# Two transformer blocks on one core: the 32-byte offset of the first projection's activations, and the placement of the tables around them

## The chip, the core and the metric

The kernel runs on one core of a Trainium2 chip. The metric is the device time of one execution in microseconds (us). Before the change it is 1629.65 us, the median of three runs (1628.27 to 1630.36).

The engines are TensorE (PE, with its weight loads shown apart as PEld), VectorE (DVE), ScalarE (ACT), GpSimd (POOL) and SyncE (SP, which here only issues transfers). On-chip memory (SBUF) has 128 partitions; an address below is the byte offset within a partition. A matmul has a stationary operand, which a weight load (LDWEIGHTS) puts into the array, and a moving operand, which streams through it. The profile names a matmul as `ps<-moving,stationary`.

## The reference

One sequence of 256 tokens with 2048 channels goes through two blocks, in float32. Cut to the products that carry the time:

```
h    = rms(x) * (1 + scale) + shift          # scale, shift, gate = silu(c) @ w_ada + b_ada
proj = h @ w_in                              # 2048 x 8192: q, k, v, z of attention; q, f, i, z of the recurrence
x    = x + gate * (concat(attention, recurrence) @ w_out)
z    = rms(x) @ w_in_2                       # second block; also rms(mem) @ w_mem_kv_2
x    = x + concat(pool, mla, cross) @ w_o_2
x    = x + (silu(conv(rms(x) @ w_gate)) * (rms(x) @ w_up)) @ w_down
```

Every large product is computed from split operands: weights and activations are each cut into a high and a low part of type fp32r, and three products (high·high, high·low, low·high) are added up in PSUM.

## The kernel before, in words

**Weights.** The weights come in pieces of 1 MB (128 partitions x 2048 values, 256 pieces) and the pieces of `w_ada` in the same size (36 through the same ring, 12 through a buffer `side`). SP loads them into a ring `raw` of 4 slots. Each piece is two halves of 1024 columns. For each half ACT writes the high part into `wh` (line 1488) and DVE the low part into `wl` (line 1886); both are rings of 4 halves. PE waits for the low part (semaphore `s_lo`) before it uses a half, ACT waits for PE before it overwrites one, and SP waits for DVE before it refills a slot of `raw`. The 512 halves are used in a fixed order.

**Activations.** A product reads its activations from one of two buffers of 16 tiles x 512 values: 256 high values of a tile, then its 256 low values. Each buffer has two names: `hA` and `hB`, and `hA2` and `hB2`, which are the same bytes begun 32 bytes later. The table `moving` says which name each stage uses. In the order of the program:

- *Memory rows* (stage B, lines 1278 to 1280, 64 matmuls each): the activations in `hB` are stationary, the weights move, 512 columns a matmul.
- *Chunks* (stage A, lines 1185 to 1187, function `chunk`): the first half of `w_in`, columns for v, the recurrence's input, q and k. The activations in `hA2` are stationary, the weights move, 512 columns. 64 halves x 12 matmuls = 768 matmuls.
- *Tiles of w_in* (stage A, lines 1138 to 1140, function `s`): the other half of `w_in`. The weights are stationary, the activations in `hA2` move, 256 columns. 32 tiles x 16 x 3 = 1536 matmuls. Between them stand the small matmuls of attention and recurrence.
- *w_out* (stage C, `hB2`), *w_in_2* (stage 2, `hA2`), latent products and *w_o_2* (stages L and D, `hB2`): the same lines 1138 to 1140, weights stationary. One short product here (lines 1161 to 1163, 8 matmuls each) has the activations stationary, from `hB2`.
- *Gate and up* (stage 3, lines 1142 and 1143): weights stationary, `hA2` moves. The high weights take one matmul of 512 columns (high and low activations at once), the low weights one of 256: 1408 pairs.
- *Down* (stage F, lines 1195 to 1197, 352 each): the activations in `hB` are stationary, the weights move, 512 columns.

**Who fills `hA2` in stage A.** ACT writes the high part (line 1547), DVE the low part (line 1940), tile by tile; PE waits for the low part of a tile the first time it reads it.

**Addresses.** The buffers are laid out one behind another in `program`, by the byte counter `at[0]`, from 16512, which is a multiple of 64. All buffers whose sizes are powers of two stay on multiples of 64; a step of 32 bytes, and the odd size of the table `vs`, shift what follows. The remainders of the start addresses, before and after the change:

| buffer | before, mod 64 / mod 128 | after, mod 64 / mod 128 |
|---|---|---|
| `raw`, `wh`, `wl`, `side`, `hA` | 0 / 0 | 0 / 0 |
| `hA2` | 32 / 32 | 32 / 32 |
| `xs` (rows of x, attention's outputs) | 32 / 32 | 0 / 64 |
| `hB` | 0 / 0 | 0 / 64 |
| `hB2`, `early` | 32 / 32 | 32 / 96 |
| `cs` (constants, with the identity) | 32 / 32 | 0 / 0 |
| `vs` (vectors of gains and biases) | 32 / 32 | 0 / 0 |
| `ones` | 0 / 0 | 32 / 96 |
| `cols`, `work` | 32 / 32 | 32 / 96 |

Slices of `hA`, `hB`, `wh` and `wl` that PE reads begin at multiples of 512 bytes from the buffer's start, so they have its remainders.

Of the kernel before, what the change touches and what calls it, by code (L numbers as in the profile page):

```python
# [7 lines left out]
F32 = mybir.dt.float32  # L8
F32R = mybir.dt.float32r
U8 = mybir.dt.uint8  # L10
ALU = mybir.AluOpType
ACT = mybir.ActivationFunctionType
AX = mybir.AxisListType

P = 128
T = 256
D = 2048
# [32 lines left out]
def _layout(table, sizes):  # L50
    at = 0
    for name, n in sizes:
        table[name] = (at, at + n)
        at += n
    return at
# [4 lines left out]
NVEC = _layout(VEC, [("norm_g", 16), ("b_ada", 48), ("g_mix", 16), ("g_ffn", 16), ("g_mem", 16),  # L60
                     ("conv_w", 132), ("conv_b", 44), ("lb", 16), ("pool_scale", 4), ("g_q_lat", 4),
                     ("g_kv_lat", 2), ("q_norm_g", 1), ("k_norm_g", 1), ("hg_norm_g", 1), ("g_q_x", 1),
                     ("g_k_x", 1), ("gq_nope", 1), ("gq_rope", 1), ("gk_nope", 1), ("gk_rope", 1), ("c", 16)])
# [743 lines left out]
class Counts:  # L807
# [8 lines left out]
    def mark(self, task, eng, step):  # L816
        name = f"{self.chain_of(task)}_{eng}"
        self.now[name] += 1
        self.found[task, eng, step] = self.now[name]
        return self.sems[name]  # L820

    def after(self, task, eng, step):
        name = f"{self.chain_of(task)}_{eng}"
        return self.sems[name], 1 if self.table is None else self.table[task, eng, step]


def program(nc, table, wts, ada, xN, xT, memN, crow, cst, vec, msk, wpool, dt, out):
    o = order()
    with ExitStack() as ctx:
        at = [nc.sbuf_base + (-nc.sbuf_base) % 32]  # L830
        ctx.enter_context(nc.sbuf_tensor("slab", [P, (nc.sbuf_top - at[0]) // 4 - 8], F32))

        def sb(name, shape, dtype=F32, size=4):
            t = nc.alloc_sbuf_tensor_at(name, shape, dtype, offset=at[0])
            at[0] += int(np.prod(shape[1:])) * size
            at[0] += (-at[0]) % 32
            return t
# [4 lines left out]
        side = nc.alloc_sbuf_tensor_at("side", [P, 4, D], F32, offset=at[0])  # L842
        hA_off = at[0]
        hA = sb("hA", [P, KT, 512], F32R)
        at[0] += 32
        xs = sb("xs", [P, KT, T])
        vs = sb("vs", [P, NVEC])
        ones = sb("ones", [P, P])
        at[0] += (hA_off - at[0]) % 2048
        early = nc.alloc_sbuf_tensor_at("early", [P, 4096], F32, offset=at[0] + 32)  # L850
        E1 = nc.alloc_sbuf_tensor_at("E1", [P, 512], F32, offset=at[0] + 32 + 15 * 2048)[:, :]
        hB_off = at[0]
        hB = sb("hB", [P, KT, 512], F32R)
        at[0] += 32
        cs = sb("cs", [P, NCST])
        mk = sb("mk", [P, len(LEVELS), P], U8, 1)
        wp = sb("wp", [P, 4, P])
        cols = sb("cols", [P, 224])
        hA2 = nc.alloc_sbuf_tensor_at("hA2", [P, KT, 512], F32R, offset=hA_off + 32)
        hB2 = nc.alloc_sbuf_tensor_at("hB2", [P, KT, 512], F32R, offset=hB_off + 32)  # L860
# [4 lines left out]
        def carve(at, *shape, of=None):  # L865
            n = int(np.prod(shape))
            assert at + n <= (NW if of is None else 4096), (at, n)
            ap = (work if of is None else of)[:, at:at + n]
            if len(shape) == 2:
                ap = ap.rearrange("p (a b) -> p a b", a=shape[0])  # L870
            if len(shape) == 3:
                ap = ap.rearrange("p (a b c) -> p a b c", a=shape[0], b=shape[1])
            return ap, at + n
# [21 lines left out]
        mark, after = counts.mark, counts.after  # L895
# [5 lines left out]
        def v_(name, i=0):  # L901
            a, _ = VEC[name]
            return vs[:, a + i:a + i + 1]
# [13 lines left out]
        xn, _ = carve(base, KT, T)  # L917
# [7 lines left out]
        hf = [ct[:, i, :] for i in range(4)]  # L925
# [49 lines left out]
        for s in range(2):  # L975
            B = {}
# [22 lines left out]
        for _ in range(2):  # L999
            m, a1 = carve(a1, T)  # L1000
            mq.append(m)
        lset = []
        for s in range(4):
            B = {}
# [16 lines left out]
        evs = [b[1] for b in o.beats if b[0] == "ev" and b[1][0] in ("g", "u")]  # L1021
        ev_no = {t: i for i, t in enumerate(evs)}
        ev_last = {"u": "mul"}
        moving = {"A": hA2, "2": hA2, "3": hA2, "B": hB, "C": hB2, "L": hB2, "D": hB2, "F": hB}
        kv_lat = {**{i: ("lkv", 1) for i in (0, 1)}, **{i: ("lq", 3) for i in (8, 9, 10, 11)}}

        def moving_ready(buf, kt):
            if buf == "A":
                return after(("xt", kt), "dve", "lo")
            if buf == "B":  # L1030
                return after(("open",), "dve", ("mlo", kt))
            if buf == "C":
                return after(("gs", kt), "dve", "lo") if kt < 8 else after(("rt", (kt - 8) // 2), "dve", "lo")
            if buf == "2":
                return after(("wo", kt), "dve", "slo")
            if buf == "L":
                return after(kv_lat[kt], "dve", ("lo", kt % 8))
            if buf == "D":
                if kt < 4:
                    return after(("pf", kt), "dve", "lo")  # L1040
                return after(("mla", kt - 4) if kt < 12 else ("mem", kt - 12), "dve", "lo")
            if buf == "3":
                return after(("o2", kt), "dve", "slo")
            return after(("hs", kt), "dve", "lo")
# [16 lines left out]
        def bank_clear(tile):  # L1061
            if tile[0] == "pf":
                return after(tile, "dve", "scale")
            if tile[0] in ("qm", "km"):
                return set_done(*tile)
            if tile[0] in M_TILES:
                return after(tile, "dve" if tile[0] == "mv" else "act", "c1")
            if tile[0] in ACT_TILES:
                return after(tile, "act", "ev")
            return after(tile, "dve", "rm" if tile[0] in RMS_TILES else "add")  # L1070
# [53 lines left out]
        def _(e):  # L1124
# [41 lines left out]
            def chunk(h, g, kt, pair, fresh):  # L1166
                n, kts = GROUPS[g]
                e.wait_ge(s_lo, h + 1)
                if fresh:
                    e.wait_ge(*moving_ready("A", kt))  # L1170
                for i in (1, 0) if g == 0 and kt == kts[0] and pair == 0 else (0, 1):
                    c = 2 * pair + i
                    w1, w2 = wh[:, h % WS, i * 512:(i + 1) * 512], wl[:, h % WS, i * 512:(i + 1) * 512]
                    if kt == kts[0]:
                        if g == 0 and c in (1, 2):
                            e.wait_ge(*after(("open",), "act", ("xc", 7)))
                        elif g == 0:
                            e.wait_ge(*bank_clear(o.prev[SET_TILES[n][c]]))
                        else:
                            e.wait_ge(*after(("part", g - 1), "act" if g < 3 else "dve", c))  # L1180
                    for t in range(2):
                        hi = hA2[:, kt, t * P:(t + 1) * P]
                        lo = hA2[:, kt, T + t * P:T + (t + 1) * P]
                        po = ps[SET_BANKS[c][t]][:, :]
                        e.matmul(po, hi, w1, start=kt == kts[0], stop=False)  # L1185
                        e.matmul(po, hi, w2, start=False, stop=False)  # L1186
                        m = e.matmul(po, lo, w1, start=False, stop=kt == kts[-1])  # L1187
                m.then_inc(s_half)
# [294 lines left out]
        def _(e):  # L1483
# [52 lines left out]
            def x_value(kt):  # L1536
                t = ("xt", kt)
                m, c = mod[:, 16 + kt:17 + kt], mod[:, kt:kt + 1]
                e.wait_ge(*after(("ada", 0, kt), "dve", "ttr"))
                e.activation(m, m, ACT.Identity, scale=v_("norm_g", kt), bias=gb[:, kt:kt + 1]).then_inc(mark(t, "act", "m"))  # L1540
                e.activation(c, c, ACT.Identity, bias=v_("b_ada", kt)).then_inc(mark(t, "act", "c"))
                e.wait_ge(*after(t, "act", "c"))
                e.wait_ge(*after(("open",), "act", ("xc", 7)))
                if kt >= 4:
                    e.wait_ge(*after(("xt", kt - 4), "dve", "lo"))
                e.activation(hf[kt % 4], xn[:, kt, :], ACT.Identity, scale=m, bias=c).then_inc(mark(t, "act", "h"))
                e.activation(hA2[:, kt, 0:T], xn[:, kt, :], ACT.Identity, scale=m, bias=c).then_inc(mark(t, "act", "hi"))

            def bounds():
                t = ("bounds",)  # L1550
# [331 lines left out]
        def _(e):  # L1882
# [54 lines left out]
            def x_low(kt):  # L1937
                t = ("xt", kt)
                e.wait_ge(*after(t, "act", "hi"))
                e.tensor_tensor(hA2[:, kt, T:2 * T], hf[kt % 4], hA2[:, kt, 0:T].bitcast(F32), ALU.subtract).then_inc(mark(t, "dve", "lo"))  # L1940

            def bounds():
                t = ("bounds",)
# [656 lines left out]
```

## Time and profile before

| | |
|---|---|
| median of three runs | 1629.65 us |
| the profiled execution's own time | 1630.36 us |
| its span in the profile | 1628.3 us, 24289 instructions |
| PE busy | 1583.3 us (97%), 9650 matmuls |
| PEld busy | 1403.4 us (86%) |
| DVE busy | 1151.7 us (71%) |
| ACT busy | 860.7 us (53%) |
| POOL busy | 137.7 us (8%) |
| chain that ended last | PE 83%, DVE 9%, ACT 4%, issue 2%, POOL 2% |
| transfers | 331.02 MB, mean 203 GB/s |
| granted TensorE clock over the span | 0.99 of full speed |

The span is the time from the first to the last instruction of the profiled execution; its own time lies 2.1 us above. Matmuls overlap in the profile: each row's duration runs from its start to the arrival of its last result, while the next has long begun. What a matmul costs in a dense stretch is therefore read from one start to the next, not from its duration.

### The profile page before, as it was taken

To read this page: it belongs to the slowest core of one execution; us is meant where nothing else is said; L and a number is where in the kernel's file an instruction comes from. 1 tells how busy PE (TensorE), PEld (TensorE's weight loads), DVE (VectorE), ACT (ScalarE), POOL (GpSimd) and SP (SyncE) were. 2 spreads that over 40 slices of the span, in tenths; PEclk is the share of its full clock that TensorE was granted. 3 is DMA by queue.
4 is the path that set the end of the run, shared out by engine and by line. 5 is a ranking of instruction groups with operands and counts; after the bars stand their busy time and mean duration, and the time that the engine had idled before them with its cause. 6 is when DMAs were issued, how large, how long until landed. Compare 5 with 4: busy or idle time off the path is not lost.

```text
span 1628.3 us, 24289 instructions
## 1 busy us (share of the span) xinstructions
PE 1583.3 (97%) x9650; PEld 1403.4 (86%) x9650; DVE 1151.7 (71%) x1696; ACT 860.7 (53%) x1321; POOL 137.7 (8%) x164
## 2 busy tenths in 40 slices
PE   8999999988999999898999999999999999999999
PEld 6788889987999999886789888888888888888887
DVE  5888858877778976656677777777777777555544
ACT  6766447677665555454556554544444444444442
POOL 0000000312120320031414000000000000000000
PEclk9999999999999999998999999999999999999999
DMA  9999965513556864432234445555545545555552
GB/s 376 357 360 366 380 248 216 207 65 129 198 189 250 326 219 157 152 130 78 104 130 156 167 173 203 185 184 201 194 176 199 196 175 199 207 183 205 185 202 104
DMA packets 47825, 331.02 MB, mean 203 GB/s; under 512 B 5281, under 2 KB 6689, under 8 KB 8417
## 3 DMA queue, kind: packets, MB, share of 16 engines
q1 hardware_dynamic: 45184, 312.20, 52.5%
q0 software_dynamic: 2240, 17.04, 2.7%
q8 instruction: 76, 1.25, 0.3%
q14 instruction: 35, 0.29, 0.1%
q10 hardware_dynamic: 290, 0.25, 0.1%
HBM read 327.37 MB, written 2.10 MB: 202 GB/s over the span
## 4 chain that ended last, share of the span: by engine, by line
PE 83%; DVE 9%; ACT 4%; issue 2%; POOL 2%; ACTq 0%; DVEq 0%; POOLq 0%
PE ps L1142 19%; PE ps L1143 10%; PE ps L1138 6%; PE ps L1140 6%; PE ps L1139 6%; PE ps L1197 5%; PE ps L1195 5%; PE ps L1196 5%; PE ps L1185 4%; PE ps L1187 4%; PE ps L1186 4%; DVE wl L1886 3%; ACT wh L1488 2%; DVE raw L1932 1%; PE ps L1320 1%
## 5 line engine op out<-in xcount | busy, mean ns | idle before, releaser
L1886 DVE TENSOR_TENSOR wl<-raw,wh 128x1024 fp32r<-128x1024 f32 x512 | 624.0, 1232 | 347.9 <-ACT wh L1488 347.5
L1488 ACT ACTIVATE wh<-raw 128x1024 fp32r<-128x1024 f32 x512 | 531.0, 1054 | 365.0 <-PE ps L1197 130.6
L1142 PE MATMUL ps<-hA,wh 128*128 128x512 f32 x1408 | 490.2, 391 | 0.0
L1143 PE MATMUL ps<-hA,wl 128*128 128x256 f32 x1408 | 397.8, 283 | 0.0
L1142 PEld LDWEIGHTS ps<-hA,wh 128*128 128x128 f32 x1408 | 265.0, 188 | 55.6
L1143 PEld LDWEIGHTS ps<-hA,wl 128*128 128x128 f32 x1408 | 266.8, 190 | 0.0
L1138 PE MATMUL ps<-hA,wh 128*128 128x256 f32 x752 | 218.8, 291 | 0.0
L1140 PE MATMUL ps<-hA,wl 128*128 128x256 f32 x752 | 210.5, 280 | 0.0
L1139 PE MATMUL ps<-hA,wh 128*128 128x256 f32 x752 | 210.3, 280 | 0.0
L1138 PE MATMUL ps<-hB,wh 128*128 128x256 f32 x576 | 166.8, 290 | 5.9 <-issue 2.5
L1139 PE MATMUL ps<-hB,wh 128*128 128x256 f32 x576 | 162.6, 282 | 0.0
L1140 PE MATMUL ps<-hB,wl 128*128 128x256 f32 x576 | 162.5, 282 | 0.0
L1138 PEld LDWEIGHTS ps<-hA,wh 128*128 128x128 f32 x752 | 142.1, 189 | 1.8 <-issue 1.2
L1139 PEld LDWEIGHTS ps<-hA,wh 128*128 128x128 f32 x752 | 142.1, 189 | 0.8 <-issue 0.2
L1140 PEld LDWEIGHTS ps<-hA,wl 128*128 128x128 f32 x752 | 141.8, 189 | 0.0
L1195 PE MATMUL ps<-wh,hB 128*128 128x512 f32 x352 | 137.0, 389 | 0.0
L1196 PE MATMUL ps<-wl,hB 128*128 128x512 f32 x352 | 136.9, 389 | 0.0
L1197 PE MATMUL ps<-wh,hB 128*128 128x512 f32 x352 | 136.9, 389 | 0.0
L1138 PEld LDWEIGHTS ps<-hB,wh 128*128 128x128 f32 x576 | 110.1, 191 | 11.4 <-issue 6.0
L1139 PEld LDWEIGHTS ps<-hB,wh 128*128 128x128 f32 x576 | 110.2, 191 | 0.4 <-issue 0.2
L1140 PEld LDWEIGHTS ps<-hB,wl 128*128 128x128 f32 x576 | 110.1, 191 | 0.0
L1185 PE MATMUL ps<-wh,hA 128*128 128x512 f32 x256 | 101.3, 396 | 1.0 <-DVE wl L1886 1.0
(287 smaller groups left out, 2072.7 us busy)
## 6 DMA issues: line engine op xcount, KB each, us to landing
raw<-in_wts SPq DMA_DIRECT2D x256, 1024.0 KB, 4.8
raw<-in_ada SPq DMA_DIRECT2D x36, 1024.0 KB, 5.4
side<-in_ada POOLq DMA_DIRECT2D x12, 1024.0 KB, 8.8
work<-in_memN SPq DMA_DIRECT2D x2, 1024.0 KB, 8.8
xs<-in_xN POOLq DMA_DIRECT2D x1, 2048.0 KB, 19.2
xs<-in_xT POOLq DMA_DIRECT2D x2, 1024.0 KB, 6.2
out_rows<-xs SPq DMA_DIRECT2D x8, 256.0 KB, 2.5
wp<-in_dt SPq DMA_DIRECT2D x8, 128.0 KB, 2.3
```

The source lines that it names most:

```text
L1138: e.matmul(po, w1, hl[:, 0:T], start=first, stop=False)
L1139: e.matmul(po, w1, hl[:, T:2 * T], start=False, stop=False)
L1140: i = e.matmul(po, w2, hl[:, 0:T], start=False, stop=last)
L1142: e.matmul(ps[bank][:, :], w1, hl, start=first, stop=False)
L1143: i = e.matmul(ps[bank][:, T:2 * T], w2, hl[:, 0:T], start=False, stop=last)
L1185: e.matmul(po, hi, w1, start=kt == kts[0], stop=False)
L1186: e.matmul(po, hi, w2, start=False, stop=False)
L1195: e.matmul(po, hi, w1, start=first, stop=False)
L1196: e.matmul(po, hi, w2, start=False, stop=False)
L1197: return e.matmul(po, lo, w1, start=False, stop=last)
L1488: e.activation(wh[:, h % WS, :], raw[:, n % RAW, part * HALF:(part + 1) * HALF], ACT.Copy).then_inc(s_hi)
L1886: e.tensor_tensor(wl[:, h % WS, :], src, wh[:, h % WS, :].bitcast(F32), ALU.subtract).then_inc(s_lo)
```

## The change

The table `moving` gives stage A the name `hA` in place of `hA2`, and the six other places that write or read the buffer in stage A follow: ACT's high part, DVE's low part, and the stationary operands of `chunk`. Stages 2 and 3 stay on `hA2`, and C, L and D on `hB2`.

The layout changes with it. The gap behind `hA` and the one behind `hB` grow from 32 to 64 bytes. `vs` and `ones` move from behind `xs` to places behind `cs` and `wp`. The line that rounded the start of `hB` so that it stood at the same remainder mod 2048 as `hA` is gone; `hB` now starts 64 bytes past that remainder. The order of instructions on every engine, their shapes and their waits are the same; only addresses differ.

```diff
@@ program @@
         hA_off = at[0]
         hA = sb("hA", [P, KT, 512], F32R)
-        at[0] += 32
+        at[0] += 64
         xs = sb("xs", [P, KT, T])
-        vs = sb("vs", [P, NVEC])
-        ones = sb("ones", [P, P])
-        at[0] += (hA_off - at[0]) % 2048
         early = nc.alloc_sbuf_tensor_at("early", [P, 4096], F32, offset=at[0] + 32)
         E1 = nc.alloc_sbuf_tensor_at("E1", [P, 512], F32, offset=at[0] + 32 + 15 * 2048)[:, :]
         hB_off = at[0]
         hB = sb("hB", [P, KT, 512], F32R)
-        at[0] += 32
+        at[0] += 64
         cs = sb("cs", [P, NCST])
+        vs = sb("vs", [P, NVEC])
         mk = sb("mk", [P, len(LEVELS), P], U8, 1)
         wp = sb("wp", [P, 4, P])
+        ones = sb("ones", [P, P])
         cols = sb("cols", [P, 224])
@@ the table of names @@
-        moving = {"A": hA2, "2": hA2, "3": hA2, "B": hB, "C": hB2, "L": hB2, "D": hB2, "F": hB}
+        moving = {"A": hA, "2": hA2, "3": hA2, "B": hB, "C": hB2, "L": hB2, "D": hB2, "F": hB}
@@ PE, chunk @@
-                        hi = hA2[:, kt, t * P:(t + 1) * P]
-                        lo = hA2[:, kt, T + t * P:T + (t + 1) * P]
+                        hi = hA[:, kt, t * P:(t + 1) * P]
+                        lo = hA[:, kt, T + t * P:T + (t + 1) * P]
@@ ACT @@
-                e.activation(hA2[:, kt, 0:T], xn[:, kt, :], ACT.Identity, scale=m, bias=c).then_inc(mark(t, "act", "hi"))
+                e.activation(hA[:, kt, 0:T], xn[:, kt, :], ACT.Identity, scale=m, bias=c).then_inc(mark(t, "act", "hi"))
@@ DVE @@
-                e.tensor_tensor(hA2[:, kt, T:2 * T], hf[kt % 4], hA2[:, kt, 0:T].bitcast(F32), ALU.subtract).then_inc(mark(t, "dve", "lo"))
+                e.tensor_tensor(hA[:, kt, T:2 * T], hf[kt % 4], hA[:, kt, 0:T].bitcast(F32), ALU.subtract).then_inc(mark(t, "dve", "lo"))
```

## Rows read from the trace of the kernel before

**Rows 1.** The page, chain that ended last, shares of the span by engine.
```profile
PE 83%; DVE 9%; ACT 4%; issue 2%; POOL 2%; ACTq 0%; DVEq 0%; POOLq 0%
```

**Rows 2.** Busy us (and count) of each engine by stage, clock, DMA share, GB/s.
```profile
66.00:110.00 44.00, 42.97 (x186) 34.40 (x185) 41.17 (x43) 30.73 (x51) 1.59 (x3) 1.00 0.90 342
110.00:200.00 90.00, 90.00 (x387) 72.55 (x386) 76.20 (x73) 48.03 (x72) 0.00 (x0) 1.00 0.97 375
200.00:249.00 49.00, 49.00 (x211) 39.48 (x210) 29.33 (x33) 21.39 (x23) 0.00 (x0) 1.00 0.68 246
249.00:540.00 291.00, 276.98 (x2258) 268.84 (x2257) 227.36 (x411) 193.06 (x311) 49.53 (x61) 0.99 0.51 184
1385.00:1628.00 243.00, 239.71 (x1058) 198.03 (x1056) 120.96 (x125) 98.98 (x114) 0.00 (x0) 1.00 0.51 182
```

**Rows 3.** Timeline of PE in the chunks: start us, us, engine, line, operands, shape.
```profile
129.81 0.40 PE L1185 MATMUL ps<-wh,hA 128*128 128x512 f32 x1
...
131.21 0.40 PE L1185 MATMUL ps<-wh,hA 128*128 128x512 f32 x1
```

**Rows 4.** Timeline of PE in the down stage.
```profile
1399.84 0.39 PE L1197 MATMUL ps<-wh,hB 128*128 128x512 f32 x1
...
1401.20 0.39 PE L1197 MATMUL ps<-wh,hB 128*128 128x512 f32 x1
```

**Rows 5.** Four lines of PE: count, duration ns min/median/max, first and last start.
```profile
L1185 PE MATMUL ps<-wh,hA x256: 395/396/469, 70.2 to 248.8; 128*128 128x512 f32 x128
...
L1195 PE MATMUL ps<-wh,hB x352: 389/389/473, 1385.1 to 1623.9; 128*128 128x512 f32 x176
...
L1278 PE MATMUL ps<-wh,hB x64: 389/389/796, 16.5 to 68.4; 128*128 128x512 f32 x64
...
L1161 PE MATMUL ps<-wh,hB x8: 395/440/628, 691.6 to 766.4; 128*128 128x512 f32 x8
```

**Rows 6.** Timeline of PE in gate and up.
```profile
899.72 0.39 PE L1142 MATMUL ps<-hA,wh 128*128 128x512 f32 x1
...
900.76 0.39 PE L1142 MATMUL ps<-hA,wh 128*128 128x512 f32 x1
```

**Rows 7.** Timeline of PE in the tiles of w_in.
```profile
259.78 0.28 PE L1139 MATMUL ps<-hA,wh 128*128 128x256 f32 x1
...
263.28 0.28 PE L1139 MATMUL ps<-hA,wh 128*128 128x256 f32 x1
```

**Rows 8.** Waits from 66 to 249 us: who for whom, us in total, times, longest.
```profile
ACT wh L1488 <- DMA raw<-in_wts: 42.3, 15, 5.3
...
ACT wh L1488 <- PE ps L1187: 31.1, 21, 1.7
...
PE ps L1185 <- DVE wl L1886: 1.0, 1, 1.0
```

**Rows 9.** Busy time by stretch: the opening, for the rate of the transfers.
```profile
16.00:66.00 50.00, 49.17 (x228) 40.49 (x228) 40.16 (x52) 35.43 (x50) 5.46 (x10) 1.00 0.98 392
```

**Rows 10.** DVE's halves, near 203 us: start us, us, line, operands.
```profile
202.12 1.23 DVE L1886 TENSOR_TENSOR wl<-raw,wh 128x1024 fp32r<-128x1024 f32 x1 [1.69 <-ACT wh L1488]
```

**Rows 11.** Timeline of PE at the same moment.
```profile
204.71 0.40 PE L1185 MATMUL ps<-wh,hA 128*128 128x512 f32 x1
```

**Rows 12.** Groups by line and shape on DVE: count, busy us, mean ns, idle before.
```profile
L2341 DVE TENSOR_TENSOR hB<-work,hB 128x256 fp32r<-128x256 f32 x44 | 18.5, 421 | 7.7 <-ACT hB L1852 7.7
...
L1940 DVE TENSOR_TENSOR hA<-work,hA 128x256 fp32r<-128x256 f32 x16 | 6.7, 420 | 0.0
```

**Rows 13.** Transposes of xs, 16 in a row: start us, us from first to last.
```profile
53.49 1.91 PE L1264 MATMUL ps<-cs,xs 128*128 128x128 f32 x16
```

**Rows 14.** Waits of PE from 249 to 540 us, the longest two.
```profile
PE ps L1320 <- DVE work L2038: 2.7, 2, 1.7
PE ps L1320 <- ACT work L1598: 2.6, 1, 2.6
```

## Prediction

> **What bounds the kernel now.** I read the chain that ended last first: 83% of it is PE, 9% DVE, 4% ACT [rows 1]. No instruction, shape or wait is changed, only addresses, so the question is whether an address changes how fast an engine goes, and whether that engine is PE where it changes. The table by stage comes next [rows 2]. In the chunks PE is busy 90.00 of 90 us (110 to 200) and 49.00 of 49 (200 to 249); in the tiles of w_in and what goes with them 276.98 of 291; in the down stage 239.71 of 243. Durations of overlapping matmuls don't tell their cost, so the third view is the timeline, where I take the distance of starts in a dense stretch at a granted clock of 1.00 (2.4 GHz):
>
> - chunks: six steps from 129.81 to 131.21, 1.40 / 6 = 233.3 ns for 512 columns [rows 3]. Stationary operand at remainder 32 (mod 64), moving operand at 0.
> - down stage: six steps from 1399.84 to 1401.20, 1.36 / 6 = 226.7 ns for 512 columns [rows 4]. Stationary 0, moving 0.
> - gate and up: three pairs from 899.72 to 900.76, 1.04 / 3 = 346.7 ns for 768 columns [rows 6]. Stationary 0, moving 32.
> - tiles of w_in: 30 steps from 259.78 to 263.28, 3.50 / 30 = 116.7 ns for 256 columns [rows 7]. Stationary 0, moving 32.
>
> Columns alone at 2.4 GHz would take 213.3, 213.3, 320.0 and 106.7 ns. What lies on top is 20.0, 13.3, 26.7 for a pair (13.3 each) and 10.0 ns.
>
> **The first step: a stationary operand at remainder 32 costs 6.7 ns more a matmul.** Chunks and down stage run the same shape, weights at remainder 0 moving in both. They differ in the stationary buffer's remainder, but also in the load beside them (DMA share 0.97 against 0.51, DVE 76.20 of 90 us against 120.96 of 243 [rows 2]). Two other lines part these. The memory rows at 16 to 68 us read `hB` (remainder 0) with a DMA share of 0.98 [rows 9] and have a median of 389 ns, as the down stage has; the eight products of line 1161 read `hB2` (remainder 32) at 692 to 766 us and have a minimum of 395, as the chunks have, with 395 to 396 [rows 5]. So the 6 to 7 ns follow the address and not the neighbours. In the chunks 768 matmuls move from 32 to 0: 768 x (233.3 - 226.7) = 5.1 us, all on PE, which is full there.
>
> The Trainium skill speaks against this step. "SBUF — State Buffer", section "Who interferes with whom", has PE's two read ports independent and says that PE and ACT never wait on anyone; "TensorE: Matmul & The Clock Gate", section "Back-to-back issue gap", gives a gap that depends on columns alone, 512 / 2.4 + 2.5 = 215.8 ns. By these an address costs nothing and the change gives 0. The rows don't agree: none of the 512-column streams is at 215.8, and two that differ in address are 6.7 apart. That rule is a rival below.
>
> **What eats of the 5.1 us: the supply of weights.** From 66 to 200 us the DMA engines are busy 0.90 to 0.97 of the time [rows 2], and ACT waits 42.3 us for pieces of weights, against 31.1 us for PE to free a half [rows 8]. PE itself waits only 1.0 us there [rows 8]. The closest moment is at 204.71 us, when PE begins a half whose low part was ready at 202.12 + 1.23 = 203.35, 1.4 us ahead [rows 10, 11]. At that point some 50 halves of 12 matmuls have gone by, 50 x 12 x 6.7 ns = 4.0 us. If the arrivals stood still, PE would wait 4.0 - 1.4 = 2.6 us there, and never get it back. They don't stand still: part of the ring's pace is PE's own (those 31.1 us), and 375 GB/s must rise only to 375 x 233.3 / 226.7 = 386, which is below the 392 of the opening [rows 9]. Ends 0 and 2.6; I take 0.5, near the lower, because the rate has been shown.
>
> **The second step: the tiles of w_in.** 1536 matmuls keep their stationary operand at 0, while the moving one goes from 32 to 0. No row of before has 256 moving columns at remainder 0. The nearest rows on the role of the moving operand are gate and up against the down stage: moving at 32 and at 0, both 13.3 ns a matmul on top [rows 4, 6]. I take 0. From above: the 10.0 ns could rise to the 20.0 of the chunks, 1536 x 10.0 = 15.4 us. From below: to nothing on top at all, again 15.4 us, now gained; nearer is the 3.3 ns by which 10.0 and 13.3 differ, 5.1 us either way. PE is busy in 95% of this stretch, with waits for DVE and ACT of at most 2.7 us in total each [rows 2, 14], so nearly all of such a step would reach the end.
>
> **The third step: the rest that moves.** `hB` keeps its remainder mod 64 but goes from 0 to 64 mod 128, `hB2` from 32 to 96. If 64 is what counts, nothing happens; all rows stand at 0 or 32, so they can't tell. I take 0, with 8.3 us as the upper end (next part). `ones`, stationary in 88 small matmuls, goes from 0 to 32, `xs`, stationary in 96 transposes, from 32 to 0. At 6.7 ns each that is 0.6 us lost and 0.6 gained, and the transposes, 16 in 1.91 us or some 109 ns apart [rows 13], may be bound by their weight loads, so that nothing comes back. I take 0, ends -0.6 and +0.6. DVE and ACT write the buffer at 0 instead of 32: DVE's sum of 256 columns takes 421 ns into `hB` at remainder 0 and 420 into `hA2` at 32 [rows 12]. Nothing there. Transfers into `xs`, `cs` and `vs` land at another remainder; no row prices that, and they lie in stretches where the engines of the DMA have the weights to bring as well. 0.
>
> **Sum.** -5.1 + 0.5 + 0 + 0 = -4.6 us. The profiled execution took 1630.36 us, 2.1 above its span of 1628.3; by the sum it becomes 1625.8. The median of the runs is 0.7 lower, 1629.65, and becomes 1625.1. I start between them, from 1629.9, and give 1625.3. A difference below 0.2% (3.3 us) is about what a measurement of this kernel can't tell from no change.
>
> **Rivals.**
>
> *A, the moving operand takes it back.* Everything measured with both operands at 0 has 13.3 ns on top. The 256-column stream at moving 32 has only 10.0. If the 10.0 is a merit of the 32 bytes between the two streams, it becomes 13.3 and the tiles go from 116.7 to 120.0: 1536 x 3.3 = 5.1 us lost, against 5.1 gained. For it: the 3.3 ns want an explanation. Against it: gate and up has the same 32 bytes and no such merit. -5.1 + 0.5 + 5.1 = +0.5: 1630.4.
>
> *B, slower.* The same place, another price: the narrow stream, in which weight load and moving columns are equally long, pays the full 6.7 ns when both begin at the same remainder. 1536 x 6.7 = 10.2 us; -5.1 + 0.5 + 10.2 = +5.6: 1635.5. It decides from 4.6 us / 1536 = 3.0 ns a matmul on, that is, above 119.7 ns the kernel is no longer faster at all. Against it: down stage and memory rows have the same remainders for both streams and are the fast ones.
>
> *C, slower by `hB`.* If what counts is the remainder mod 128, the down stage's 1056 and the memory rows' 192 matmuls pay 6.7 ns: 1248 x 6.7 = 8.3 us; -4.6 + 8.3 = +3.7: 1633.6.
>
> *D, both streams gain.* The narrow stream has its 3.3 ns less with an aligned moving operand: -4.6 - 5.1 = -9.7: 1620.2. For it: the chunks show that an operand pays for starting at 32; against it: gate and up again.
>
> *E, an address costs nothing*, the skill's rule, with the 6.7 ns due to something in the chunks that stays. 0: 1629.9. Against it stand lines 1278 and 1161 [rows 5].
>
> **How the numbers follow.** Forecast 0.42, A 0.26, D 0.09, B 0.12, C 0.08, E 0.03. Of the forecast's 0.42 some 0.06 lose over 1.3 us to the supply and end within 0.2%. Faster by over 0.2%: 0.36 + 0.09 = 0.45. Within: 0.06 + 0.26 + 0.03 = 0.35. Slower: 0.12 + 0.08 = 0.20. The forecast's own range is 1624.5 (nothing lost) to 1628 (2.6 lost and 0.6 of small ones). The range for 8 in 10 takes in A and C and most of D's price, and leaves out B: 1620.5 to 1634.
>
> **What would show it.** In the profile after: the chunks' matmuls at 389 ns and 226.7 apart, and the stage some 5 us shorter; if 395 and 233.3 stay, the first step is wrong. PE's waits for DVE at lines 1185 and following, up to 200 us, give the supply's part: 1.0 us now, up to 3.6. The tiles of w_in at 116.7 apart (forecast), 120.0 (A), over 119.7 (B) or below 114 (D). The down stage at 226.7 (forecast) or 233.3 (C). Gate and up must stay at 346.7 a pair. The forecast is wrong if the tiles' distance moves by more than 1 ns or so, since 1536 of them weigh twice as much as the 768 of the chunks.

## The result, and the profile after

The changed kernel takes 1641.01 us, median of four runs (1639.46 to 1643.21), against 1629.97 in the same sitting. The ratio is 1.0062 (95% interval 1.0044 to 1.0080): 10 to 11 us slower, where 4.6 us faster was forecast, and beyond the range.

The profiled execution has a span of 1637.0 us against 1628.3. That execution itself took 1638.8 us, a little less than the four. Where the 8.7 us came in, from the first matmul of a stage to the first of the next, in us; the two right columns belong to experiments below:

| stage | before | after | stage A alone | layout alone |
|---|---|---|---|---|
| opening, memory rows | 70.2 | 70.0 | 70.1 | 70.3 |
| chunks | 179.3 | 179.2 | 177.8 | 179.8 |
| tiles of w_in | 255.7 | 259.4 | 258.9 | 255.5 |
| w_out to w_o_2 | 383.3 | 384.1 | 383.3 | 384.3 |
| gate and up | 496.6 | 494.1 | 495.0 | 494.2 |
| down | 243.2 | 250.2 | 243.2 | 250.1 |
| span | 1628.3 | 1637.0 | 1628.4 | 1634.2 |

Gate and up have the same addresses in all four and still differ by 2.4 us: so much of one profile is no evidence. (So the 0.8 us of the stages from w_out to w_o_2 are none either.) The tiles (+3.7) and the down stage (+7.0) are above it.

The timeline of PE after the change answers to [rows 3, 4, 7]; the lines of the kernel have numbers lower by one. First the chunks and the down stage:

```profile
129.73 0.39 PE L1186 MATMUL ps<-wh,hA 128*128 128x512 f32 x1
...
131.09 0.39 PE L1186 MATMUL ps<-wh,hA 128*128 128x512 f32 x1
...
1399.69 0.39 PE L1195 MATMUL ps<-wl,hB 128*128 128x512 f32 x1
...
1401.09 0.39 PE L1195 MATMUL ps<-wl,hB 128*128 128x512 f32 x1
```

Six steps each: 1.36 / 6 = 226.7 ns in the chunks (233.3 before), 1.40 / 6 = 233.3 in the down stage (226.7 before). The two have changed places. Then the tiles of w_in and, from `hB2`, those of w_out:

```profile
259.75 0.28 PE L1138 MATMUL ps<-hA,wh 128*128 128x256 f32 x1
...
263.35 0.28 PE L1138 MATMUL ps<-hA,wh 128*128 128x256 f32 x1
...
539.78 0.28 PE L1138 MATMUL ps<-hB,wh 128*128 128x256 f32 x1
...
543.38 0.28 PE L1138 MATMUL ps<-hB,wh 128*128 128x256 f32 x1
```

Thirty steps in 3.60 us: 120.0 ns in both, against 116.7. The memory rows follow the down stage, by their durations against the 389/389 of [rows 5]:

```profile
L1277 PE MATMUL ps<-wh,hB x64: 393/394/795, 16.5 to 68.3; 128*128 128x512 f32 x64
```

The chunks' faster matmuls shortened their stage by 0.1 us. The table by stage, as [rows 2], and the waits from 66 to 249 us, as [rows 8]:

```profile
66.00:110.00 44.00, 43.19 (x190) 35.38 (x189) 41.18 (x43) 30.32 (x50) 1.58 (x3) 1.00 0.88 341
110.00:200.00 90.00, 87.28 (x379) 70.43 (x378) 73.50 (x72) 48.01 (x71) 0.00 (x0) 1.00 0.95 364
```
```profile
ACT wh L1487 <- DMA raw<-in_wts: 43.9, 16, 5.5
...
ACT wh L1487 <- PE ps L1186: 27.2, 17, 1.7
...
PE ps L1184 <- DVE wl L1885: 2.5, 5, 0.8
...
PE ps L1184 <- ACT xs L1669: 1.2, 1, 1.2
```

PE is busy 87.28 of 90 us where it was 90.00. Its named waits are 3.7 us against 1.0, of which 0.8 and 1.0 stand ahead of the stage's first matmul. The longest single gap is not a wait for weights. It stands ahead of the stage's matmul 337, where PE waits until ACT has copied a partial sum out of PSUM (line 1669):

```profile
146.05 0.39 PE L1186 MATMUL ps<-wh,hA 128*128 128x512 f32 x1
147.60 0.47 PE L1184 MATMUL ps<-wh,hA 128*128 128x512 f32 x1 [1.17 <-ACT xs L1669]
```

ACT begins that copy at 146.41 us, only 0.5 us earlier than before the change (146.91), while PE would be there at 146.28 instead of 148.71. All distances between starts that are longer than usual, late weight loads included, add 4.8 us to the dense stream, against 0.1 before: 1.4 at this gap, 3.3 where PE comes to a half whose weights are late. The transfers move 364 GB/s, not the 386 that I had asked of them.

### The profile page after: what moved, and what is told of

Read it like the earlier page. It is cut to its first block, busy times and chain, and to the rows that moved or that the text cites. A ratio compares the mean times of both kernels' runs of the same rounds, so it can differ in the third digit from the quotient of the medians.

```text
span 1637.0 us, 24289 instructions
## 1 busy us (share of the span) xinstructions
PE 1593.5 (97%) x9650; PEld 1409.5 (86%) x9650; DVE 1151.3 (70%) x1696; ACT 860.6 (53%) x1321; POOL 137.5 (8%) x164
## 4 chain that ended last, share of the span: by engine, by line
PE 77%; DVE 12%; ACT 5%; issue 3%; DMA 1%; POOL 1%; ACTq 0%; DVEq 0%; POOLq 0%
PE ps L1141 19%; PE ps L1142 10%; PE ps L1137 7%; PE ps L1139 7%; PE ps L1138 7%; PE ps L1196 5%; PE ps L1195 5%; PE ps L1194 5%; DVE wl L1885 4%; DVE raw L1931 3%; ACT wh L1487 2%; DMA raw<-in_wts 1%; PE ps L1319 1%; PE ps L1277 1%; PE ps L1184 1%
## 5 line engine op out<-in xcount | busy, mean ns | idle before, releaser
L1196 PE MATMUL ps<-wh,hB 128*128 128x512 f32 x352 | 139.2, 395 | 0.0
L1194 PE MATMUL ps<-wh,hB 128*128 128x512 f32 x352 | 139.2, 395 | 0.0
```

The costliest lines, as they stand in the source:

```text
L1194: e.matmul(po, hi, w1, start=first, stop=False)
L1196: return e.matmul(po, lo, w1, start=False, stop=last)
```

## The experiments

**Two parts of the change, each alone.** Stage A alone on the old layout:

```diff
-        moving = {"A": hA2, "2": hA2, "3": hA2, "B": hB, "C": hB2, "L": hB2, "D": hB2, "F": hB}
+        moving = {"A": hA, "2": hA2, "3": hA2, "B": hB, "C": hB2, "L": hB2, "D": hB2, "F": hB}
```
(with the chunks' operands, ACT's and DVE's line as in the change)

> The kernel before with stage A alone moved from hA2 to hA; the layout stays. Theory 1: chunks 226.7 ns, tiles of w_in 120.0, down stage and memory rows 226.7 and w_out 116.7 as before. The chunks' 5.1 us go to the wait for weights, as in the changed kernel, where that stage ended 0.3 us earlier only; the tiles lose about 4 us (their stage took 259.4 us against 255.7 there). So 1633 to 1634 us against 1630. Rival (the loss of the changed kernel comes from stage A): 1641. Rival (a matter of the layout alone): 1630.

Measured: 1629.87 against 1629.03, ratio 1.0008 (0.9996 to 1.0019). Chunks 226.9 ns apart, tiles 119.8, down stage 226.7, w_out 116.7. The distances are as expected in every stage; the time is not: 1633 to 1634 had been expected. Of the chunks' 5.1 us 1.5 were won, where none had been expected; the tiles' +3.2 us stand against them and against a gate and up that is 1.6 us shorter in this profile, which is no evidence.

The layout alone (the changed kernel with the five lines of stage A put back to `hA2`):

> The changed kernel with stage A back on hA2; the new layout stays, with hB at 64 and hB2 at 96 mod 128. Theory 1: chunks 233.3 and tiles 116.7 as before; memory rows and down stage 233.3, w_out, latent products and w_o_2 120.0. Down stage 1056 x 6.7 = 7.0 us longer, the 1728 narrow matmuls on hB2 3.3 ns each, 5.8 us, of which the changed kernel showed some 2 to 3. So 1637 to 1642 us. Rival (the remainder mod 64 is what counts): 1630.

Measured: 1635.67, ratio 1.0038 (1.0024 to 1.0052), +6.6 us. Down stage 233.3 apart, w_out 120.0, chunks 233.3, tiles 116.7. So most of the loss sits in the layout, and there in the down stage (+6.9 us in the profile). Its median duration is 393 ns, against 389 before [rows 5]:

```profile
L1194 PE MATMUL ps<-wh,hB x352: 393/393/400, 1384.1 to 1629.8; 128*128 128x512 f32 x176
```

Both parts add up to 7.5 us, the whole change shows 10. The intervals are 2 to 3 us wide to each side, so this doesn't contradict them; it is not explained either.

**Is it the remainder mod 128?** That was my theory after the result, and `hB` was moved 64 bytes on:

```diff
+        at[0] += (hA_off - at[0]) % 128
         early = nc.alloc_sbuf_tensor_at("early", [P, 4096], F32, offset=at[0] + 32)
```

> The changed kernel with 64 bytes more ahead of hB, which then starts at 0 mod 128 (but 128 past hA mod 2048). Theory 1: as the kernel with stage A alone moved: down stage 226.7, w_out 116.7, chunks 226.7, tiles 120.0, 1633 to 1634 us. Rival (hB must stand at the same remainder as hA mod 2048, or the new places of xs, cs, vs and ones cost): 1641 as the changed kernel, down stage 233.3.

Measured: 1639.49, ratio 1.0066 (1.0049 to 1.0083). The down stage stayed at 232.4 ns. The theory fell: `hB` was at 0 mod 128 from the weights and still slow. (The profiled execution was the longest of its six, 1643.65 us.)

```profile
L1196 PE MATMUL ps<-wl,hB x352: 390/393/404, 1392.9 to 1637.6; 128*128 128x512 f32 x176
```

**The cost by itself.** A kernel with PE alone, 24 matmuls a group, each group with other start offsets. In outline:

```
for a in (0, 32, 64, 96, 128, 160, 192, 224, 256, 512, 1024):      # stationary, bytes
    for b in (0, 32, 64, 96, 128, 256):                            # moving, bytes
        24 x matmul(512 moving columns); 24 x matmul(256 moving columns)
```

> A kernel of its own: after one load of weights PE alone runs groups of 24 matmuls of type fp32r from SBUF, 128 stationary columns, moving 512, moving 256, and then 512 and 256 in turn. Each group has another pair of start offsets from a multiple of 2048: stationary 0 to 1024, moving 0 to 256. It computes nothing of the reference. Theory 1 (the cost depends on the offset of both streams mod 128, nothing beside PE is needed for it): with 512 moving columns at offset 0, 226.7 ns a matmul at stationary 0 and 233.3 at 32 and 64; with 256 moving columns and stationary 0, 116.7 at moving 32 and 120.0 at 0 and 96; the value at stationary 128, 256, 512, 1024 is that of 0. Theory 2 (it depends on the distance of the two streams only): stationary 32 with moving 32 is as fast as 0 with 0. Rival (the differences come from ACT, DVE or the transfers beside PE, or from the absolute place of the buffers): all groups of one width show one value.

The timeline of it: start, length, and x24 for a group; the groups of the offsets (stationary, moving) = (0, 0), (0, 32), (0, 64), and then (32, 0), (32, 32).

```profile
22.55 5.60 PE L60 MATMUL ps<-wfull,hfull 128*128 128x512 f32 x24
27.99 3.04 PE L62 MATMUL ps<-wfull,hfull 128*128 128x256 f32 x24
30.86 5.76 PE L60 MATMUL ps<-wfull,hfull 128*128 128x512 f32 x24
36.46 2.96 PE L62 MATMUL ps<-wfull,hfull 128*128 128x256 f32 x24
39.26 5.66 PE L60 MATMUL ps<-wfull,hfull 128*128 128x512 f32 x24
44.76 2.88 PE L62 MATMUL ps<-wfull,hfull 128*128 128x256 f32 x24
47.48 5.77 PE L60 MATMUL ps<-wfull,hfull 128*128 128x512 f32 x24
...
72.76 5.75 PE L60 MATMUL ps<-wfull,hfull 128*128 128x512 f32 x24
78.35 3.01 PE L62 MATMUL ps<-wfull,hfull 128*128 128x256 f32 x24
81.19 5.62 PE L60 MATMUL ps<-wfull,hfull 128*128 128x512 f32 x24
86.65 3.04 PE L62 MATMUL ps<-wfull,hfull 128*128 128x256 f32 x24
89.52 5.76 PE L60 MATMUL ps<-wfull,hfull 128*128 128x512 f32 x24
```

A group's cost is the way to the next group's start over 24. For 512 columns: (27.99 - 22.55) / 24 = 226.7 ns at (0, 0), 233.3 at (0, 32), 229.2 at (0, 64), 232.9 at (32, 0), and 227.5 at (32, 32). For 256 columns: 119.6, 116.7, 113.3, 118.3, and 119.6. So (32, 32) is as (0, 0): for these pairs it is the distance of the two streams that counts, not where one of them stands. Without the step between groups the values in ns by distance (moving minus stationary, mod 256) are, each the same within 1 ns for most of its pairs:

| distance | 0 | 32 | 64 | 96 | 128 | 160 | 192 | 224 |
|---|---|---|---|---|---|---|---|---|
| 512 columns | 226.7 | 233.3 | 228.9 | 233.9 | 233.5 | 234.3 | 233.3 | 232.9 |
| 256 columns | 120.0 | 116.7 | 113.3 | 119.9 | 118.7 | 117.5 | 113.4 | 118.6 |

A stationary operand at 256, 512 or 1024 gives the values of 0 in both rows. For 512 columns no pair is more than 1.5 ns from another of its distance. For 256 columns two distances have two values each: at 64 six of nine pairs take 113.3 ns and three 117.9, at 192 four of six take 113.5 to 113.9 and two 117.8. One of the three is (192, 0), the second row here:

```profile
324.62 5.67 PE L60 MATMUL ps<-wfull,hfull 128*128 128x512 f32 x24
330.12 2.99 PE L62 MATMUL ps<-wfull,hfull 128*128 128x256 f32 x24
332.95 5.76 PE L60 MATMUL ps<-wfull,hfull 128*128 128x512 f32 x24
```

(332.95 - 330.12) / 24 = 117.9 ns. So theory 2 of the expectation holds, with a period of 256 bytes, for 512 columns and for 256 columns at the distances that the kernels before and after use (0, 32 and 96), not for 256 columns at 64 and 192. It accounts for the kernel: chunks 224 before, 0 after; down stage 0 before, 192 after, 128 in the third experiment (232.4); tiles 32 before, 0 after; w_out 32 before, 96 after. Nothing beside PE was running, so neither transfers nor ACT or DVE are the cause.

A second sweep used the kernel's own order of operands:

> A kernel of its own, as the first sweep, with PE alone; it computes nothing of the reference. The three kinds of stream of the kernel in its own order of operands: narrow (weights stationary, 256 activations moving), pair (512, then 256 moving) and wide (activations stationary, 512 weights moving), each at 17 distances of the two streams, 0 to 256 bytes in steps of 16. Theory (only the distance mod 256 counts): narrow 120.0 ns at 0, 116.7 at 32, 113.3 at 64, 119.9 at 96, as in the first sweep; pair 346.7 at 32 and 352 to 354 at 0; wide 226.7 at 0 and 233.3 at 32 and 64, 232.4 at 128; the value at 256 is that of 0. Rival (the order of the operands, two matmuls with the same weights in a row, matters): narrow at 32 or 64 comes out otherwise than in the first sweep.

| distance of h from w | 0 | 16 | 32 | 64 | 96 | 112 | 128 | 160 | 192 | 224 | 240 | 256 |
|---|---|---|---|---|---|---|---|---|---|---|---|---|
| narrow, ns | 120.0 | 118.6 | 116.7 | 117.8 | 120.0 | 113.3 | 118.3 | 117.4 | 113.3 | 118.4 | 117.1 | 119.7 |
| pair, ns | 353.3 | 346.7 | 347.0 | 348.9 | 349.9 | 353.3 | 350.6 | 346.7 | 352.3 | 346.7 | 351.7 | 346.7 |
| wide, ns | 228.1 | 226.7 | 233.3 | 233.3 | 234.3 | 233.3 | 233.3 | 233.3 | 228.9 | 233.3 | 226.7 | 226.7 |

These are 12 of its 17 distances. Here h is stationary in the wide stream and moves in the other two. The values at 0, 32 and 96 are those of the kernels. At 64 the narrow stream costs 117.8, not 113.3. That could be the order of operands, as the rival had it, but the first sweep has both values at this distance without any change of order, so the rival is not shown; what chooses between the two is open. At 0 the pair has two values as well, 353.3 here and 346.6 in the first sweep with the stationary operand at 512.

**Gate and up at distance 0**, `"3": hA` in the table `moving`, nothing else:

> The kernel before with gate and up alone moved from hA2 to hA, distance 0 instead of 32. Theory of the distance: a pair takes 353 to 354 ns instead of 346.7, 1408 x 6.2 to 7.3 = 8.7 to 10.3 us longer, 1638 to 1640. Rival (the moving operand's place costs nothing, as forecast): 1629.

Measured: 1628.61 against 1628.33, ratio 1.0001 (0.9987 to 1.0015); 346.9 ns a pair. The kernel shows the lower of the two values, so the sweep's 353.3 did not carry over, and my expectation was wrong.

**The narrow stages at 64**, written before the second sweep was known (`hA` and `hB` with names 64 bytes on for A, 2, C, L and D):

> The kernel before with the moving activations of the narrow stages (w_in, w_out, w_in_2, latent products, w_o_2) 64 bytes past the start of the weights' remainder instead of 32; gate and up stay at 32, down stage and memory rows at 0. Theory of the distance: narrow matmuls 113.3 ns apart instead of 116.7, chunks 233.3 as before. 3984 narrow matmuls x 3.3 = 13.3 us on PE; of the 5.1 in the tiles of w_in some two thirds arrived when they went the other way, of the 5.8 on hB2 about 1. So 1619 to 1626 us against 1629. Rival (a distance that is a multiple of 64 is bad, as the changed kernel's 64 for the down stage was): narrow 120, 1635 or more.

Measured: 1630.86 against 1628.33, ratio 1.0012 (1.0001 to 1.0024), slightly slower where 1619 to 1626 had been expected. Once more, for its profile:

> The kernel of e4_plus_64 once more for its profile. Narrow matmuls at 117.8 ns as in the second sweep at 64 (not 113.3 as in the first), chunks 233.3: the 0.1% by which it was slower. Rival: 116.7 and the rest is waits.

```profile
259.74 0.28 PE L1139 MATMUL ps<-hA,wh 128*128 128x256 f32 x1
...
263.27 0.28 PE L1139 MATMUL ps<-hA,wh 128*128 128x256 f32 x1
```

3.53 / 30 = 117.7 ns: the higher of the two values that the sweeps have at 64, and 1 ns over the 116.7 at distance 32.

**What holds the chunks back.** On the kernel with stage A alone, the pieces of `w_ada` were loaded to half their width, then to 64 of 2048 columns (what both compute is not the reference's):

```diff
-                e.dma_start(raw[:, n % RAW, :], src).then_inc(raw_in[n % RAW], 16)
+                w = 1024 if o.entries[n][0] == "a" else 2048        # then 64
+                e.dma_start(raw[:, n % RAW, 0:w], src[:, 0:w]).then_inc(raw_in[n % RAW], 16)
```

> The kernel with stage A alone moved, in which each of the 36 pieces of w_ada that go through the ring raw is loaded to half its width; the rest of the slot keeps older values, so scale and shift are not the reference's. DVE and ACT do the same work. Theory (the transfers hold the chunks back): PE's waits in the chunks fall from 3.5 us to under 1 and the stage takes 174 to 175 us instead of 177.8. Rival (DVE, ACT or the depth of the rings hold it back): 177.8 as before.

> The kernel with stage A alone moved, in which the 36 pieces of w_ada in the ring raw are loaded to 64 of 2048 columns; scale and shift are not the reference's, DVE and ACT work as before. Theory (transfers hold the chunks back, by rate or by the time to land): PE's waits in the chunks under 0.5 us (3.5 with whole pieces, 3.0 with half), stage 174 to 175 us. Rival (DVE's work of 2.3 us a piece in the order in which it stands between the halves): still about 3 us of waits, 177 to 178.

Measured, chunks' stage and the excess over the dense stream: 177.8 us and 3.5 with whole pieces, 177.1 and 3.0 with half, 175.9 and 1.7 with 64 columns. Rows of the last one:

```profile
110.00:200.00 90.00, 88.80 (x391) 72.95 (x391) 76.23 (x75) 49.16 (x73) 0.00 (x0) 1.00 0.58 206
```
```profile
ACT wh L1489 <- DMA raw<-in_wts: 34.9, 11, 5.8
...
PE ps L1186 <- ACT xs L1671: 1.2, 1, 1.2
PE ps L1186 <- DVE wl L1887: 1.0, 1, 1.0
```
```profile
145.85 0.39 PE L1188 MATMUL ps<-wh,hA 128*128 128x512 f32 x1
147.44 0.47 PE L1186 MATMUL ps<-wh,hA 128*128 128x512 f32 x1 [1.20 <-ACT xs L1671]
```

The excess has two parts, and they behave differently. Of the 1.7 us that are left 1.5 are the gap ahead of matmul 337, where PE waits for ACT's copy of the partial sum (line 1671 here). It is in every profile with fast chunks, and the bytes do not move it: 1.4 us in the changed kernel, 1.4 with stage A alone, 1.5 with half pieces and with thin ones. The other part is the late halves of weights: 3.3, 2.1, 1.4 and 0.1 us in the same order. With thin pieces (DMA engines busy 0.58 instead of 0.96, 206 GB/s instead of 366) they are gone; the 1.0 us for DVE stands ahead of the stage's first matmul. So for the late halves the theory holds in its extreme, though it isn't shown whether by the rate or by the time that a piece of `w_ada` takes to land (median 2.5 us with thin pieces, 5.7 with whole ones); half pieces prove little, since the four profiles with whole pieces have 2.1 to 5.2 us of late halves. ACT still waits 34.9 us for weights with thin pieces without holding PE up by it. Why ACT comes to the copy no earlier was not tried: with thin pieces it begins it at 146.24 us.

None of this reaches the time of the whole kernel: 1631.17 against 1628.33 us with half pieces (ratio 1.0021) and 1629.55 against 1628.03 with thin ones (1.0010), where whole pieces had 1.0008.

**hB at the weights' remainder mod 256.** The changed kernel once more, with the line of the third experiment, `% 256` in place of `% 128`, and 32 bytes less behind `hB`:

> The changed kernel with hB moved on to the weights' remainder mod 256 (not mod 2048). Theory of the distance mod 256: down stage 226.7, w_out 116.7, memory rows 226.7, chunks 226.7, tiles of w_in 120.0, so as the kernel with stage A alone moved, 1629 to 1631. Rival (xs, cs, vs and ones at their new places, or the rounding mod 2048, cost too): 1634 or more.

Measured: 1630.25 against 1628.03, ratio 1.0014 (1.0000 to 1.0029); down stage 226.7 ns, w_out 117.0.

```profile
L1196 PE MATMUL ps<-wl,hB x352: 389/389/395, 1392.1 to 1630.9; 128*128 128x512 f32 x176
```

The time of the runs is that of stage A alone. The edit does not part `hB` from the tables: `cs`, `vs` and `ones` start elsewhere than before, but at the same remainders mod 256 as before (32, 32 and 128 from the weights), and only `xs` stays at 64 instead of 32. What ties the loss to `hB` is the down stage of the profiles: 243.2 us before, 250.2 in the changed kernel, 243.2 here. This profiled execution was the longest of its ten, 1637.21 us. Its chunks' stage had 6.5 us of excess, 3.7 of them around the same wait for ACT:

```profile
148.79 0.39 PE L1187 MATMUL ps<-wh,hA 128*128 128x512 f32 x1
151.07 0.48 PE L1185 MATMUL ps<-wh,hA 128*128 128x512 f32 x1 [1.89 <-ACT xs L1670]
...
152.20 0.63 PE L1185 MATMUL ps<-wh,hA 128*128 128x512 f32 x1
152.62 0.63 PE L1186 MATMUL ps<-wl,hA 128*128 128x512 f32 x1
```

After this gap of 2.28 us from start to start, in which PE did nothing, the granted clock was at 0.5 (1.2 GHz) for some matmuls, which are 427 ns apart. After the 1.59 us of the profile with thin pieces it stayed at 1.00.

**A layout from the sweep.** A, 2, C, L and D 192 bytes past the weights' remainder mod 256, gate and up at 32, memory rows and down stage at 0:

```diff
+        w_at = at[0]
+        cols = sb("cols", [P, 224])
+        at[0] += (w_at + 192 - at[0]) % 256
...
         hA_off = at[0]
         hA = sb("hA", [P, KT, 512], F32R)
+        hA2 = nc.alloc_sbuf_tensor_at("hA2", [P, KT, 512], F32R, offset=hA_off + 96)
+        at[0] += 96
...
+        at[0] += (w_at + 192 - at[0]) % 256
+        hB2 = sb("hB2", [P, KT, 512], F32R)
+        hB = nc.alloc_sbuf_tensor_at("hB", [P, KT, 512], F32R, offset=hB_off + 64)
...
+        moving = {"A": hA, "2": hA, "3": hA2, "B": hB, "C": hB2, "L": hB2, "D": hB2, "F": hB}
```

> The kernel before with the layout made by the sweep: the name that stages A, 2, C, L and D use begins 192 bytes past the weights' remainder mod 256, gate and up at 32, down stage and memory rows at 0. Theory (what the sweep by distance shows carries over): chunks 228.9 ns apart instead of 233.3, narrow matmuls 113.3 instead of 116.7, the rest unchanged. On PE 768 x 4.4 = 3.4 us and 3984 x 3.3 = 13.3 us; by the shares that earlier kernels showed to arrive (about 1.5 us at most of the chunks, two thirds of 5.1 in the tiles of w_in, all of 2.4 in w_in_2, 1 of the rest) 6 to 9 us: 1619 to 1623 against 1628.5. Rival (the sweep's 113.3 at 192 is a state of PE alone that ACT, DVE and transfers disturb): narrow at 116 to 120, 1626 to 1632.

Measured: 1625.94 against 1628.03, ratio 0.9983 (0.9968 to 0.9998): 2.1 us in the medians, faster than both kernels, but by less than the 6 to 9 us expected, and close to what the rival gave. Chunks and narrow matmuls:

```profile
129.75 0.39 PE L1187 MATMUL ps<-wh,hA 128*128 128x512 f32 x1
...
131.12 0.39 PE L1187 MATMUL ps<-wh,hA 128*128 128x512 f32 x1
...
869.82 0.28 PE L1141 MATMUL ps<-hB,wh 128*128 128x256 f32 x1
...
873.22 0.28 PE L1141 MATMUL ps<-hB,wh 128*128 128x256 f32 x1
```

1.37 / 6 = 228.3 ns (228.9 in the sweep), and 3.40 / 30 = 113.3 at this place. Over a whole stage the narrow ones average 115.6 in the tiles of w_in and 115.0 to 116.3 later: in the tiles 724 of 1493 are 112 to 114 ns apart and 466 are 118 to 120 (counted over the whole stage), so the rival holds in part; the first sweep has both values at this distance too. And the chunks' stage took 183.1 us, longer than before, with 7.2 us of excess: 3.2 of late halves and 4.0 around the wait for ACT, 2.53 us from start to start, after which the granted clock fell to 0.5 here too. The gain came from w_out to w_o_2: 378.4 us against 383.3.

## Why the prediction was wrong

**The first step gave the right number for a wrong reason.** "A stationary operand at remainder 32 costs 6.7 ns more a matmul": the chunks did go from 233.3 to 226.7. But in all the rows that I compared [rows 3 to 5] the weights stood at 0, so the stationary remainder and the distance of the streams were the same number, and I took the one for the other. The sweep parts them: stationary 32 with moving 32 is as fast as 0 with 0 (227.3 against 226.7 to 228.1 ns). That the number came true is luck of that layout.

**The second step failed.** "The nearest rows on the role of the moving operand are gate and up against the down stage": both had 13.3 ns on top, so I took the moving operand's place as free. It is not: from 116.7 to 120.0, 3.3 ns a narrow matmul, as rival A had it, and +3.7 us of its 5.1 in the stage. The comparison went across widths, and the distance acts on each width in its own way: 32 is the best of 0, 32 and 96 for narrow ones and among the worst for 512 columns.

**The third step failed most.** "If 64 is what counts, nothing happens": `hB` at 64 from the weights cost the down stage 6.6 ns in each of 1055 intervals, 7.0 us, as rival C had it for this stage, though neither for 64 nor for 128 but for 256 bytes. I gave C a chance of 0.08 because no row spoke for it; none spoke against it either. The memory rows slowed as well (393 ns instead of 389), but their stage took 0.2 us less, so C's part for them did not arrive. The 1728 narrow matmuls on `hB2` went from 116.7 to 120.0 as well, which no rival had. Of 5.8 us the stages there show 0.8, which is within the scatter of profiles; the held-up starts on `hB2` (over 140 ns apart) add 9.3 us where they added 12.5, so waits took some 3 us of it. The rest was not traced.

**What eats of the chunks' gain was mis-sized, and one of its two parts was missing.** 0.5 us was taken, 2.6 given as the upper end. It was 4.8 in the changed kernel and 3.5 to 6.9 in four profiles with fast chunks. In the changed kernel 3.3 are late halves of weights. That the opening moves 392 GB/s did not show that the ring can; and the upper end assumed arrivals that stand still, while they came later than before: the half that PE began at 204.71 us, its low part ready at 203.35, was waited for until 205.54. The other 1.4 us are the wait for ACT's copy of a partial sum ahead of matmul 337, for which the prediction has no term: only the slack of the halves was looked at. Before the change PE came to it 1.8 us after the copy had begun (148.71, 146.91); in the changed kernel it could go on 1.2 us after that (147.60, 146.41). So the slack was some 0.6 us, while 336 matmuls at 6.7 ns bring PE there 2.25 us earlier. The 1.0 us that the prediction gives as PE's wait in the chunks stands ahead of their first matmul, at 70.23 us; inside the stage there was none.

**Rivals A and C were held apart.** I gave each its time as if the others did not occur. By its own prices both together are -5.1 + 0.5 + 5.1 + 8.3 = +8.8 us, 1638.7, where the range ended at 1634 because no case contained two of them, though nothing in them excludes each other. With what the profile showed it is -5.1 + 4.8 + 3.7 + 0.8 + 7.0 = +11.2, inside the measured interval (7 to 13 us). That sum is made afterwards from the same profile, whose own difference is 8.7: gate and up came out 2.4 us shorter in it, with no cause shown.

The Trainium skill's rule ("SBUF — State Buffer", section "Who interferes with whom": PE's two read ports are independent, and PE never waits on anyone) gives no difference at all. In the sweep PE ran alone and its 256-column matmuls took 113.3 to 120.0 ns by the distance of its own two operands. The measurement decides against reading the rule that far. The 215.8 ns of the prediction are used beyond what they are given for: the Trainium skill ("TensorE: Matmul & The Clock Gate", section "Back-to-back issue gap") calls N/2.4 + 2.5 the gap of a single isolated matmul and has weight load and matmul together set the spacing of a stream. The streams here were at 226.7 ns and above. Why the distance acts, and why with a period of 256 bytes, no run here shows.

## What to carry to other kernels

Where TensorE streams fp32r from SBUF without a gap, the distance between the start of the stationary and that of the moving operand, mod 256 bytes, is a parameter of its own: look at the distance of starts in the timeline to 1 ns before and after any change of layout, also one that only moves a table. Sweep it with the kernel's own order of operands and width, since the best distance for 512 columns (0) is a bad one for 256. A stage that is made faster can run into any wait that had slack: look at the slack of each thing that PE waits for there, not of the weights alone. Where several rivals can occur together, price them together.

## What was not expected of the hardware

- With PE alone and nothing but start offsets changed, 512-column fp32r matmuls with a weight load each cost 226.7 to 234.3 ns and 256-column ones 113.3 to 120.2, at a granted clock of 1.00 (2.4 GHz).
- One distance can have two steady values: a pair at distance 0 took 353.3 ns in one place and 346.6 in another, and 346.9 in the kernel; a 256-column matmul at 64 took 113.3 or 117.9.
- With a quarter of the ring's bytes taken away and the DMA engines' share down from 0.96 to 0.81, late halves still cost the chunks 1.4 us instead of 2.1; they were gone at a share of 0.58.
- In two profiles a gap of 2.3 and one of 2.5 us on PE were followed by the lower clock (matmuls 427 ns apart); gaps of 1.6 to 1.7 us at the same place in the others were not.
